# A fused two-block model on one NeuronCore: forget logarithms as two extra rows of the attention's operands, and modulation sums at other units

## What is computed

```python
def block_causal_attention(q, k, v, scale, key_valid, cum=None):
    ...
        s = jnp.einsum('bqhd,bkhd->bhqk', q[:, q0:q1], k[:, :q1], ...) * scale
        if cum is not None:
            s = s + (cq - ck)          # cum of the query less cum of the key, for each head
        s = jnp.where(mask[None, None], s, NEG_INF)
        p = jax.nn.softmax(s, axis=-1).astype(v.dtype)
        outs.append(jnp.einsum('bhqk,bkhd->bqhd', p, v[:, :q1]))
...
    o_mla = block_causal_attention(q, k, v, 1.0 / math.sqrt(MLA_QK_DIM), key_valid)
...
    log_f = jax.nn.log_sigmoid(f_logit + b_forget)
    cum = jnp.cumsum(log_f, axis=1)
    o_fox = block_causal_attention(fq, fk, fv, 1.0 / math.sqrt(FOX_HEAD_DIM), key_valid, cum)
```

## Time and profile before

| | |
|---|---|
| median of 3 runs | 1687.96 us (1683.99 to 1689.22) |
| the profiled execution | 1675.52 us, its span 1673.7 us |
| PE busy | 1517.0 us, 91% of the span |
| DVE, ACT, POOL busy | 1025.2, 540.3, 554.1 us |
| DMA | 571.87 MB, 342 GB/s in the mean |
| granted clock of PE, mean | 0.96 of full speed |

### The profile page before, as it was taken

How to read it: one execution, slowest core, us unless ns; L and a number is a source line. 1 busy time by engine, 2 the same in 40 slices (tenths; PEclk the granted TensorE clock), 3 DMA queues, 4 the chain that set the end, 5 groups by cost and what they waited for, 6 DMA issues and landing times.

```text
span 1673.7 us, 22767 instructions
## 1 busy us (share of the span) xinstructions
PE 1517.0 (91%) x8260; PEld 1160.3 (69%) x8260; DVE 1025.2 (61%) x2100; ACT 540.3 (32%) x1094; POOL 554.1 (33%) x361
## 2 busy tenths in 40 slices
PE   6999989999999999999999988889877878787877
PEld 6999988778899999998889986434433333333332
DVE  5554355556343325998983846667676676758556
ACT  4443353354344335443115442212121212121113
POOL 3555444000144442001001413444454535354450
PEclk9999999899999998999999999999998989899998
DMA  7667689987789997998876739999999999999995
GB/s 266 241 224 253 233 346 385 322 275 264 286 321 367 371 370 278 360 375 336 316 265 245 299 133 371 371 426 427 426 428 426 428 427 427 427 427 427 427 426 245
DMA packets 98724, 571.87 MB, mean 342 GB/s; under 512 B 10960, under 2 KB 11088, under 8 KB 48976
## 3 DMA queue, kind: packets, MB, share of 16 engines
q1 hardware_dynamic: 60768, 298.41, 49.1%
q0 software_dynamic: 36864, 268.45, 38.1%
q10 hardware_dynamic: 1008, 3.90, 0.6%
HBM read 569.68 MB, written 135.27 MB: 421 GB/s over the span
## 4 chain that ended last, share of the span: by engine, by line
PE 70%; DMA 19%; DVE 6%; issue 2%; ACT 2%; POOL 1%; ACTq 0%; POOLq 0%; DVEq 0%
DMA arena<-pairs,eidx 16%; PE ps L2262 11%; PE ps L1723 9%; PE ps L1725 9%; PE ps L1724 9%; PE ps L2068 5%; DMA ring<-pairs,eidx 2%; PE ps L2232 2%; PE ps L1774 2%; PE ps L1776 2%; PE ps L1775 2%; PE ps L2019 2%; PE ps L2085 2%; DVE arena L1619 1%; PE ps L1738 1%
## 5 line engine op out<-in xcount | busy, mean ns | idle before, releaser
L2262 PE MATMUL ps<-arena 128*128 128x512 f32 x872 | 421.6, 636 | 90.0 <-ACT arena L1053 89.8
L2262 PEld LDWEIGHTS ps<-arena 128*128 128x128 f32 x872 | 173.1, 203 | 324.4 <-issue 204.7
L1619 DVE CUSTOM_DVE_ANT_0 arena<-arena 128x1024 f32<-128x1024 f32 x218 | 265.6, 1224 | 169.3 <-DMA arena<-pairs,eidx 169.2
L660 POOL TENSOR_TENSOR w_lo<-ring,w_hi 128x1024 fp32r<-128x1024 f32 x82 | 217.2, 2650 | 427.8 <-DVE w_lo L1123 347.6
L690 POOL DMA_INDIRECT arena<-pairs,eidx x218 | 249.5, 1144 | 293.1 <-PE ps L2262 242.8
L1723 PE MATMUL ps<-u_hi,w_hi 128*128 128x256 f32 (+1 forms) x1056 | 305.3, 289 | 10.2 <-DVE u_lo L1092 10.1
L1725 PE MATMUL ps<-u_hi,w_lo 128*128 128x256 f32 (+1 forms) x1056 | 303.5, 287 | 0.0
L1724 PE MATMUL ps<-u_lo,w_hi 128*128 128x256 f32 (+1 forms) x1056 | 303.0, 287 | 0.0
L707 ACT ACTIVATE w_hi<-ring 128x1024 fp32r<-128x1024 f32 x188 | 197.9, 1056 | 170.4 <-PE ps L1776 77.5
L1723 PEld LDWEIGHTS ps<-u_hi,w_hi 128*128 128x128 f32 x1056 | 201.6, 191 | 12.9 <-issue 11.0
L1725 PEld LDWEIGHTS ps<-u_hi,w_lo 128*128 128x128 f32 x1056 | 202.3, 192 | 0.0
(11 more groups left out here) (318 smaller groups left out, 2317.8 us busy)
## 6 DMA issues: line engine op xcount, KB each, us to landing
ring<-in_stream SPq DMA_DIRECT2D x130, 1024.0 KB, 7.0
pairs<-in_peer_u SPq DMA_DIRECT2D x128, 512.0 KB, 7.5
pairs<-in_peer_v SPq DMA_DIRECT2D x128, 512.0 KB, 8.9
arena<-in_ada SPq DMA_DIRECT2D x32, 768.0 KB, 6.3
arena<-pairs,eidx POOLq DMA_INDIRECT x218, 17.2
h<-in_x_t SPq DMA_DIRECT2D x1, 1088.0 KB, 7.4
arena<-in_keys ACTq DMA_DIRECT2D x1, 1024.0 KB, 6.7
out<-arena SPq DMA_DIRECT2D x2, 512.0 KB, 5.1
```

The lines of the kernel that those rows point to most:

```text
L660: pool.tensor_tensor(lo[:, half, :], ring[:, slot, e * HALF:(e + 1) * HALF], hi[:, half, :], ALU.subtract).then_inc(used if e else lo_done, 1)
L1619: dve.tensor_tensor_reduce(row, row, hf[:, n % HEAD_ROWS // TOPK, :], 1.0, 0.0, ALU.mult, ALU.add, dots[:, n % HEAD_ROWS:n % HEAD_ROWS + 1 ...
L2262: mm = pe.matmul(ps[:, Y_BANKS[j // TOPK] + half, :], diag[:, n % DIAGS, :], slot_of(n)[:, D + half * 512:D + half * 512 + 512], start=(hd ...
```

## The change

- The cumulated logarithms, scaled, become two more rows of each fox head's queries and keys, so that the product of queries and keys adds them: a query tile has rows (cum, 1), a key tile (1, -cum). Products L1971 and L1972 and the constant `sel` go.
- `fk` gets one tile for each head instead of one for two, so it is filled by 8 operations on 64 partitions. Heads with even numbers use rows 0 to 65 (`FOX_ROWS`), odd ones all 128.
- POOL clears `fqz` and half of `fk`, sets the rows of ones, and, when DVE has the logarithms, issues 16 DMAs of one row each that put cum and -cum in place. The first fox unit waits for all 16 (`cum_in`); DVE waits for POOL's clearing (`fox_set`) before it fills `fqz`.
- The 8 late modulation sums come after n = 10, 13, 16, ... 31. SP issues 16 blocks ahead of the slices instead of 24, and 8 blocks behind them (`AFTER_ADA`).

```diff
-BEFORE_ADA = 24
+BEFORE_ADA = 16
+AFTER_ADA = 8
...
-        fk = view(HEADS // 2, T)
+        fk = view(HEADS, T)
...
+        CUM_ROWS = [slice(HD, HD + 2), slice(0, 2)]
+        FOX_ROWS = [slice(0, HD + 2), slice(0, 2 * HD)]
...
             at += (KT // 2 - 2) * ADA_Q * ADA_BLOCKS
+            for n in range(AFTER_ADA):
+                pair_up(at + n)
+            at += AFTER_ADA
...
+            pool.wait_ge(half_used, half_number(0, BASE["w_out"], 0))
+            pool.memset(fqz[:, :, :], 0.0).then_inc(fox_set, 1)
+            pool.memset(fk[0:HD, 1::2, :], 0.0).then_inc(fox_set, 1)
+            pool.wait_ge(fox_set, 2)
+            for e in range(2):
+                pool.memset(fqz[CUM_ROWS[e], e::2, :], 1.0).then_inc(fox_set, 1)
+                pool.memset(fk[CUM_ROWS[e], e::2, :], 1.0).then_inc(fox_set, 1)
+            pool.wait_ge(fox_set, 6)
+            pool.wait_ge(cum_done, 4)
+            for hd in range(HEADS):
+                row = CUM_ROWS[hd % 2].start
+                of = slice(FL_ROW + hd, FL_ROW + hd + 1)
+                pool.dma_start(fqz[row:row + 1, hd, :], cumz[of, xc]).then_inc(cum_in, 16)
+                pool.dma_start(fk[row + 1:row + 2, hd, :], ncumz[of, :]).then_inc(cum_in, 16)
...
-            then(dve.memset(cumz, 0.0), lb_step)
...
-            then(dve.memset(fqz[:, :, :], 0.0), lb_step)
...
+            dve.wait_ge(fox_set, 6)
...
-                dve.scalar_tensor_tensor(fk[:, j, :], praw[:, 8 + j, :], V("g_fk"), ps[:, FK_BANKS[j], 0:T],
-                                         ALU.mult, ALU.mult).then_inc(fox_done, 1)
+                for e in range(2):
+                    r = slice(HD * e, HD * e + HD)
+                    dve.scalar_tensor_tensor(fk[r, 2 * j + e, :], praw[r, 8 + j, :], V("g_fk")[r], ps[r, FK_BANKS[j], 0:T],
+                                             ALU.mult, ALU.mult).then_inc(fox_done, 1)
...
-            dve.tensor_scalar(ncumz, cumz, -1.0, None, ALU.mult).then_inc(cum_done, 1)
+            dve.tensor_scalar(cumz[fr, :], logf[fr, 1, :], 1.0 / FOX_SCALE, None, ALU.mult).then_inc(cum_done, 1)
+            dve.tensor_scalar(ncumz[fr, :], logf[fr, 1, :], -1.0 / FOX_SCALE, None, ALU.mult).then_inc(cum_done, 1)
...
-                if n % 2 and n >= units // 2:
-                    ada_add(KT // 2 + n // 8, n // 2 % ADA_Q)
+                if n >= units - 3 * 2 * ADA_Q and n % 3 == 1:
+                    i = (n - (units - 3 * 2 * ADA_Q)) // 3
+                    ada_add(KT - 2 + i // ADA_Q, i % ADA_Q)
...
-                        pe.wait_ge(cum_done, 3)
-                    pe.matmul(dst, fqz[:, f, q], fk[:, f // 2, 0:keys_n], start=True, stop=False)
-
-                    pe.matmul(dst, cumz[:, X0 + t * P:X0 + (t + 1) * P], C("sel")[:, f:f + 1].broadcast_to([P, keys_n]), start=False, stop=False)
-                    pe.matmul(dst, C("sel")[:, f:f + 1].broadcast_to([P, P]), ncumz[:, 0:keys_n], start=False, stop=False)
+                        pe.wait_ge(cum_in, 2 * HEADS * 16)
+                    own = FOX_ROWS[f % 2]
+                    pe.matmul(dst, fqz[own, f, q], fk[own, f, 0:keys_n], start=True, stop=False)
```

## The result

| | before | after |
|---|---|---|
| median, side by side, 20 runs each | 1688.1 us | 1693.08 us |
| ratio, 95% interval | | 1.0047 [1.0031, 1.0062] |
| profiled execution, span | 1675.52, 1673.7 us | 1691.01, 1689.2 us |
| output projection starts | 414.61 us | 406.95 us |
| first product of the second network (L1723, now L1746) | 452.63 us | 452.50 us |

The forecast was 1685.0 in a range of 1679.0 to 1690.5. The kernel became slower, by 0.5%. The profiled execution of before, 1675.52 us, is shorter than all the others of before in this comparison (1680.81 us and more).

The account below looks back on a forecast made before the run. PE alone was taken to set the pace of the fox units. The terms -8.8 + 4.2 + 0.3 + 1.3 made -3.0 us, from 1688.0 to 1685.0 us, in a range of 1679.0 to 1690.5.

Parts of the forecast that it names:

- step 5: SP's queue: 8 blocks behind the last slice make the second weight piece delay the norm, +1.3 us; later networks, gathers untouched.
- Step 1: Fox units of the attention: without the extra products each of 8 pairs falls from 5.00 to 3.90 us, -8.8 us.
- Step 2: Late modulation sums on DVE in the attention: no longer covered by PE's excess work, seven sums cost 0.6 us each, +4.2 us.
- my first rival: Attention: the scores' lead of two units hides the modulation sums, total -5.7 us, 1682.3 us; chance 0.22.
- Steps 3 and 4: Logarithms: one more scaling +0.3 us, POOL's 16 DMAs 0. Preparation: POOL's clearing and filling `fk` 0.
- The slower rival: Ahead of the first fox unit: POOL's 16 serial DMAs bring the rows late, +11 us, 1699; chance 0.08.
- The rival that DVE sets the pace: Attention: sums cost their full 6.8 us and the queue 1.5, total -0.2 us, 1687.8 us; chance 0.18.

Follow-up runs that it names:

- e2: The kernel before with only 8 more unused columns of constants, gather buffer at byte 80416; ratio to before 1.0063.
- e9: The kernel before with 16 more unused columns of constants, gather buffer at byte 80448; ratio to before 1.0045.
- e11: The kernel before with 32 more unused columns of constants, gather buffer at byte 80512; ratio to before 1.0053.
- e1: The changed kernel with 8 unused columns put back into the constants, so the gather buffer starts at its old byte; ratio to before 1.0011.
- e13: The kernel of e1 run again, beside e14 on one chip; ratio to before 1.0004.
- e6: e5 with each late modulation sum cut to 8 of its 1536 columns; one execution, 1677.66 us.
- e8: e1 with 12 blocks ahead of the slices and 12 behind, in place of 16 and 8; one execution, 1696.39 us.
- e3: e1 with all 24 blocks ahead of the slices, none behind; ratio to before 1.0002 from seven of twelve executions, the other five 1705.86 to 1712.45 us.
- e14: The kernel of e5 run again, beside e13 on one chip; ratio to before 0.9987.
- e4: e3 with the 8 late modulation sums back behind n = 17, 19, ... 31; ratio to before 1.0013.
- e5: e1 with the 8 blocks behind the last slice moved to the weights of the second block's output products; ratio to before 0.9963.
- e12: The kernel before with 64 more unused columns of constants, gather buffer at byte 80640; ratio to before 1.0004.

## Why the prediction was wrong

**The step that failed is the last sentence of step 5**, "the later networks and the gathers are untouched". I looked at the queue and not at memory. The change removes a constant, and I counted that as nothing at all. It moved the gathers' buffer off a multiple of 256 bytes. e2, e9 and e11 put the price at 1.0045 to 1.0063, from first to last gather it is about 8 us, and e1 takes it back. Without it the change has the ratio 1.0011 or 1.0004 (e1, e13), 1688.8 to 1690 against the 1688.1 of before, inside my range, 4 to 5 us above my 1685.0. The trace of before could not show this price, but the diff showed the shorter list of constants, and the queue of the gathers fills the DMA engines for 38% of the span.

**The other miss is a size in step 5:** the second piece 1.4 us late. I had its arrival right (forecast 437.2, measured 437.87), which is partly luck: the last slice was issued at 394.31 and not at 397.7, and from there the queue took 43.6 us and not 39.5. When PE wanted it I had wrong. The norm was due 7.6 us before 443.82, at 436.2, and its input was there at 441.7: 5.5 us late. Then came what I had no term for, 1.8 us of half clock in the norm's means. Together 7.3 of the 7.7 us won; with the 0.2 us that L1827 is longer 7.5. So the sum is -7.7 + 7.5 + 8.2 (the buffer's place, after against e1) = +8.0 us, and the ratio 1.0047 is 7.9. An arrival that a queue fixes gives back whatever is won ahead of it: a larger gain in the attention only made this wait longer.

**Step 1** counted -8.8; the pair went from 5.00 to 3.75 and not 3.90, so -10.0 (e6). I had said that fox pairs inherit the MLA pairs' wait. They inherit half of it: 3.75 lies between 3.59 (PE never waits) and 3.90.

**Step 2** counted +4.2; 7 x 0.31 to 0.37 is 2.2 to 2.6. The two units of lead take more than I gave them, but not all, so my first rival was nearer for this term, with three pairs of 11.98 us between its 11.7 and my 12.9. The sum of steps 1 and 2 is -7.4 to -7.8 against the 7.7 measured.

**Steps 3 and 4** hold: one scaling more is one row of 0.29 us; nobody waited for `cum_in` or for POOL's clearing, though that took 9 us and not 6.5. The slower rival (POOL's 16 DMAs, deciding from 1.4 us each) was at 0.49 and far away. The slower outcome came from a place for which I had no rival.

**The rival that DVE sets the pace** is out: DVE idles 1.92 us ahead of the soft maximum that precedes the sum of 374.76.

## What to carry to other kernels

When an edit adds or removes anything in on-chip memory, work out the new address of every buffer that large transfers write to, and keep it on a multiple of 256 bytes. This is shown here for gathered rows of 8192 bytes only; such a slowdown shows as GB/s in a stage that the diff does not touch. When a gain is made ahead of a transfer whose arrival is fixed by a queue, the gain counts only up to that arrival, and the wait can cost clock besides: in the four traces with the wait (after, e1, e8, e13) the norm's means take 5.5 to 5.8 us, in the twelve without it 3.69. And one profiled execution has its own stalls and clock: before a difference between two traces is explained, look whether an execution of the old kernel can show it too.

## What the hardware showed that I had not expected

- The place of the buffer on a partition: 427 GB/s on a multiple of 256 bytes, 420 to 421 at 32, 64, 128 and 224 bytes past one, and nothing else changed but what lies behind the constants with it.
- In e3, PE idled 2.8 us and then had half the clock for 70 us of unbroken work; in after, an idle 5.7 us was followed by half clock only within the norm, and L1827 had its pace back. The same kind of work, another outcome. And half clock comes without any idling: in the rows of before and e9 above PE is busy 4.00 of 4.00 us.
- In some traces ACT stands still at the start of the expert layer, once (8.5 us in e1 and e14) or twice, here in the chain of after:

```profile
1011.09 6.55 another core or an unknown queue
...
1017.68 4.32 another core or an unknown queue
```

The trace names no queue of this core. It costs 6.6 us (the gathers of e1 from first to last against those of before, at the same 427 GB/s), and that much of the difference of the two spans is no work of the change. It goes with the chip and not with the kernel: all six traces from the two chips of e1 to e4 and of e13 and e14 have it, e2 among them, which is the kernel before with 8 unused columns; none of the eight from the two chips of e5 to e12 has it. The lowest times of before are 1681.15 and 1681.69 us on the first two chips, 1675.57 and 1674.82 on the others. What causes it is open.
